# One more head of tile 0 as a streamed head, value rows one group later, paired forgetting scores and a fifth late head

## The reference

```
h   = x + W_out [ forgetting attention (8 heads of 64) || differential attention (4 heads of 2 x 64) ] (W_in RMSNorm(x))
h   = h + PEER(RMSNorm(h))
out = RMSNorm_final(h)

forgetting: softmax(q.k / 8 + c_q - c_k, causal) v,   c = cumsum(log sigmoid(f + b))
differential: (softmax(q1.k1 + alibi) - lambda softmax(q2.k2 + alibi)) v, chunk mask, RMSNorm of each head

PEER, for each block of 128 tokens, each of 8 heads:
  q  = xn @ w_q;  s1, i1 = top16(q1 . keys1);  s2, i2 = top16(q2 . keys2)
  16 best of the 256 sums  ->  expert numbers e (16 of 16384) and gates g = softmax(top)
  hid = gelu(u_tab[e] . xn) * g
  out += sum over the 16 of hid * v_tab[e]
```

## Time and profile before

| | |
|---|---|
| median of 3 runs | 1544.32 us |
| the profiled execution | 1543.67 us |
| its span | 1541.9 us |
| moved | 596.50 MB, 387 GB/s over the span |
| busy | PE 81%, DVE 71%, POOL 50%, ACT 30% |

### The profile page before, as it was taken

The page is one execution under the profiler, slowest core; times in us unless marked ns, Lnnn a source line. Parts: engine busy times, 40 slices in busy tenths (PEclk is TensorE's granted clock), DMA queues, the critical chain, the costliest instruction groups (busy, mean ns, idle before and its releaser), DMA issues.

```text
span 1541.9 us, 12952 instructions
## 1 busy us (share of the span) xinstructions
PE 1253.9 (81%) x3663; PEld 654.6 (42%) x3663; DVE 1097.3 (71%) x2538; ACT 459.2 (30%) x1188; POOL 771.6 (50%) x653
## 2 busy tenths in 40 slices
PE   9999978897787829899978777787787777878767
PEld 8776645574444514444433333333333233333323
DVE  3257799998998987666666676666666766666654
ACT  3432254446524312222222222222122322222222
POOL 0026587777568754345455444445544454444540
PEclk9999988898998959999999989989999999899998
DMA  9669899999899999999999999999999999999994
GB/s 385 258 254 414 341 322 367 372 382 318 277 363 337 401 388 422 421 422 421 421 423 421 422 421 422 422 421 422 421 422 421 422 421 421 421 422 421 421 421 182
DMA packets 102045, 596.50 MB, mean 387 GB/s; under 512 B 11736, under 2 KB 11736, under 8 KB 46680
## 3 DMA queue, kind: packets, MB, share of 16 engines
q0 software_dynamic: 92160, 536.91, 86.2%
q1 hardware_dynamic: 9816, 58.77, 9.5%
HBM read 593.54 MB, written 2.10 MB: 386 GB/s over the span
## 4 chain that ended last, share of the span: by engine, by line
DMA 39%; PE 16%; DVE 5%; POOL 2%; ACT 2%; issue 2%; DVEq 0%
PE acc L968 14%; DMA map_mem<-in_peer_uv_dram,eidx 8%; DMA v_all<-in_peer_uv_dram,eidx 8%; DMA mix_mem<-in_peer_uv_dram,eidx 6%; DMA u_ring<-in_peer_uv_dram,eidx 5%; DMA v_ring<-in_peer_uv_dram,eidx 4%; DMA w_ring<-in_peer_uv_dram,eidx 4%; DMA act_mem<-in_peer_uv_dram,eidx 3%; PE mm L764 1%; ACT diag L1202 1%; DVE map_mem L1521 1%; PE sc L764 1%; DVE v_all L1521 1%; POOL v_ring L685 1%; DMA v_ring<-in_peer_v_dram,eidx 1%
## 5 line engine op out<-in xcount | busy, mean ns | idle before, releaser
L1195 ACT ACTIVATE gel<-hid 128x4 f32<-128x4 f32 x126 | 25.9, 205 | 786.5 <-DVE hid L1521 686.3
L678 POOL DMA_INDIRECT u_ring<-in_peer_u_dram,eidx x128 | 157.4, 1230 | 173.7 <-DVE eidx L1501 98.5
L685 POOL DMA_INDIRECT v_ring<-in_peer_v_dram,eidx x128 | 155.1, 1212 | 60.9 <-issue 31.7
L968 PE MATMUL acc<-v_all,diag 128*128 128x512 f32 x240 | 123.5, 663 | 67.6 <-ACT diag L1202 35.7
L1549 DVE SCALAR_TENSOR_TENSOR h<-v_ring,coef,h 128x1024 f32<-128x1024 f32 x128 | 164.4, 1284 | 10.3 <-DMA v_ring<-in_peer_v_dram,eidx 6.9
L1513 DVE CUSTOM_DVE_ANT_0 u_ring<-u_ring,hn 128x1024 f32<-128x1024 f32 x128 | 155.9, 1218 | 20.1 <-DMA u_ring<-in_peer_u_dram,eidx 19.9
L968 PE MATMUL acc<-map_mem,diag 128*128 128x512 f32 x240 | 119.9, 647 | 24.6 <-ACT diag L1202 24.6
L968 PE MATMUL acc<-v_ring,diag 128*128 128x512 f32 x240 | 116.8, 632 | 25.9 <-ACT diag L1202 21.4
L968 PE MATMUL acc<-u_ring,diag 128*128 128x512 f32 x240 | 115.6, 627 | 27.0 <-ACT diag L1202 27.0
L1202 ACT ACTIVATE diag<-ident,coef 128x128 f32<-128x128 f32 x376 | 121.0, 390 | 33.3 <-DVE coef L1539 27.4
L699 POOL DMA_INDIRECT v_all<-in_peer_uv_dram,eidx x60 | 70.0, 1166 | 91.1 <-PE acc L968 85.3
(11 more groups left out here) (282 smaller groups left out, 2328.4 us busy)
## 6 DMA issues: line engine op xcount, KB each, us to landing
w_ring<-in_slabs_dram SPq DMA_DIRECT2D x29, 1024.0 KB, 8.2
v_ring<-in_slabs_dram SPq DMA_DIRECT2D x6, 1024.0 KB, 10.6
u_ring<-in_slabs_dram SPq DMA_DIRECT2D x6, 1024.0 KB, 10.9
map_mem<-in_slabs_dram SPq DMA_DIRECT2D x6, 1024.0 KB, 8.1
h<-in_x_dram SPq DMA_DIRECT2D x4, 512.0 KB, 12.5
u_ring<-in_peer_u_dram,eidx POOLq DMA_INDIRECT x128, 7.1
v_ring<-in_peer_v_dram,eidx POOLq DMA_INDIRECT x128, 7.3
v_all<-in_x_cols_dram SPq DMA_DIRECT2D x3, 512.0 KB, 7.4
```

The source lines that it names most:

```text
L678: nc.gpsimd.indirect_dma_start(out=u_ring[:, c % U_RING, :], out_offset=None, in_=peer_u[0], in_offset=bass.IndirectOffsetOnAxis(ap=eidx[n ...
L685: nc.gpsimd.indirect_dma_start(out=v_ring[:, c % V_RING, :], out_offset=None, in_=peer_v[0], in_offset=bass.IndirectOffsetOnAxis(ap=eidx[n ...
L968: last = nc.tensor.matmul(acc[half][:, :], diag[:, c % COLS, :], v_row(n, c)[:, half * BANK:(half + 1) * BANK], start=first, stop=(n % PH ...
L1195: nc.scalar.activation(gel[:, par, g0:g0 + COLS], hid[:, par, g0:g0 + COLS], ACT.Gelu).then_inc(gelu_done, 1)
```

## The change

- `HOSTS = 1` becomes `HOST_HEADS = 7`: the eighth head of tile 0 (n = 7) is a streamed head. Its v rows go to `acc` instead of `h`; `fin_tile` adds both as before, now at n = 8. Its first matmul starts the banks, so DVE no longer clears them; PE waits for what DVE waited for.
- `SLOTS` becomes 28. With the fifth late head out of the list, shares of 533.0 stand over 27 groups, 19.7 to a group.
- `BEHIND = 2`: DVE adds group k-2 beside the dots of group k, ACT does the GELU of group k-1 at gap 4 of group k, and POOL issues v rows four places later. DVE works the last two hosted groups of adds off in the first streamed group.
- The order of the places changes: six are free early (`FREE_ROWS`), and rows of n = 7 are gathered from the last hosted group on.
- Forgetting scores come in pairs at even steps: both 64-row matmuls, then both 40-row matmuls.
- `LATE_HEADS` = 5.

```diff
-HOSTS = 1
+HOST_HEADS = 7
-LATE_HEADS = 4
+LATE_HEADS = 5
+BEHIND = 2
-    SLOTS = HOSTS * PH * GRP
+    SLOTS = HOST_HEADS * GRP
...
-        row_mem = [m for flat in (v_flat, map_mem, ur_flat, vr_flat) for m in halves_of(flat)]
-        EARLY_ROWS = len(row_mem) - 4
+        row_mem = [m for flat in (v_flat, map_mem) for m in halves_of(flat)]
         row_mem += [store[:, 0:PH * 2 * K1], mix_mem[:, :]]
+        FREE_ROWS = len(row_mem)
+        row_mem += [m for flat in (ur_flat, vr_flat) for m in halves_of(flat)]
...
+        def group_at(k):
+            return k // GRP, k // GRP % 2, k % GRP * COLS
...  gather_row, POOL
-                elif place == EARLY_ROWS:
+                elif place == 0:
+                    pool.wait_ge(pv_done, len(item_list))
+                elif place == FREE_ROWS - 1:
+                    pool.wait_ge(mm_full, mm_done(("mixT", TILES - 1, 1)))
+                elif place == FREE_ROWS:
                     pool.wait_ge(dot_done, HOSTED)
+                elif place == FREE_ROWS + 2:
                     pool.wait_ge(v_used, HOSTED)
...  POOL's order
+            for n in range(HOST_HEADS):
                 for c in range(TOPK):
                     ahead = TOPK * n + c + COLS
                     if ahead < HOSTED:
                         ...
                         gather_u(ahead // TOPK, ahead % TOPK)
-                    gather_v(n, c)
+                    elif ahead - HOSTED < FREE_ROWS:
+                        if ahead == HOSTED:
+                            numbers_of(HOST_HEADS)
+                        gather_row(HOST_HEADS, ahead - HOSTED)
+                    if TOPK * n + c >= (BEHIND - 1) * COLS:
+                        gather_v(*divmod(TOPK * n + c - (BEHIND - 1) * COLS, TOPK))
+            for c in range(COLS, FREE_ROWS):
+                gather_row(HOST_HEADS, c)
+            for i in range(HOSTED - (BEHIND - 1) * COLS, HOSTED):
+                gather_v(*divmod(i, TOPK))
...  PE
+            def pair_scores(g, step):
+                t, first = at_step(g, 0, step)
+                nk, j = P * (t + 1), GROUPS[g].index(t)
+                if first == 0:
+                    pe.wait_ge(selq_ready, 2 * (t + 1))
+                both = [(HD * (m % 2), m // 2, map_no[(t, m)]) for m in (first, first + 1)]
+                for lo, ch, k in both:
+                    if k >= len(sc_b):
+                        pe.wait_ge(sc_drained, k + 1 - len(sc_b))
+                    nc.tensor.matmul(sc_b[k % len(sc_b)][:, 0:nk], qT[lo:lo + HD, ...], kv_t[lo:lo + HD, ...],
+                                     start=True, stop=False)
+                for lo, ch, k in both:
+                    nc.tensor.matmul(sc_b[k % len(sc_b)][:, 0:nk], selq[lo:lo + 40, ...], caug[lo:lo + 40, 0:nk],
+                                     start=False, stop=True).then_inc(sc_full, 1)
...  first streamed group, PE
-                    first = n % PH == 0 and c == 0
-                    if first:
+                    first = (n == HOST_HEADS or n % PH == 0) and c == 0
+                    if first and n == HOST_HEADS:
+                        pe.wait_ge(*emptied(MM[MM_HOSTED - 1]))
+                        ...
+                        pe.wait_ge(sc_drained, len(map_list))
+                    elif first:
                         pe.wait_ge(acc_drained, 2 * (n // PH))
...  ACT, hosted
-                            if gap == 2 * COLS - 2:
-                                gelu(n, n % 2, grp * COLS)
+                        if gap == COLS and (n or grp):
+                            gelu(*group_at(GRP * n + grp - 1))
...  DVE, hosted
-                        behind = ((k - 1) // GRP, (k - 1) // GRP % 2, (k - 1) % GRP * COLS)
+                    behind = group_at(k - BEHIND)
...
-                for half in range(2):
-                    link(nc.vector.memset(acc[half][:, :], 0.0))
...  DVE, first streamed group
+                    if n == HOST_HEADS and grp == 0:
+                        for k in range(GRP * HOST_HEADS - BEHIND, GRP * HOST_HEADS):
+                            behind = group_at(k)
+                            coefs(*behind)
+                            for c in range(COLS):
+                                if k == GRP * HOST_HEADS - BEHIND:
+                                    row_dot(n, par, c)
+                                add_row(behind[0], behind[1], behind[2] + c)
```

More of the change, by code:

```diff
@@ L459, in build @@
         place_rows, places = {}, []
-        for i in range((HEADS - PH * HOSTS) * TOPK):
+        for i in range((HEADS - HOST_HEADS) * TOPK):
             if i < FULL_FROM:
@@ L571, in slab_view @@
             return w.rearrange("p (c n) -> p c n", c=KC)
[L573 removed]
+        HOSTED = HOST_HEADS * TOPK
         def row_place(n, c):
@@ L711, in _ @@
                 gather_u(0, c)
-            for n in range(PH * HOSTS):
+            for n in range(HOST_HEADS):
                 for c in range(TOPK):
@@ L977, in _ @@
                 piece(*p_)
[L978 to L984, removed]
+            for n in range(HOST_HEADS):
+                for grp in range(GRP):
+                    for gap in range(GAPS):
+                        for p_ in pieces_in(n, grp, gap):
+                            piece(*p_)
+            for n in range(HOST_HEADS, HEADS):
                 for grp in range(GRP):
                     peer_group(n, grp * COLS)
-                    k = GRP * (n - PH * HOSTS) + grp
+                    k = GRP * (n - HOST_HEADS) + grp
                     if k in LATE_PE:
@@ L1238, in _ @@
             gate_exp(0)
[L1239 to L1242, removed]
-                            if gap == 2 * COLS - 2:
-                                gelu(n, n % 2, grp * COLS)
-                            for p_ in pieces_in(n, grp, gap):
-                                piece(*p_)
-                        if tile and n == PH * tile and grp == 0:
-                            fin_rt(tile - 1)
-                        if grp == 2:
-                            gate_exp(n + 1)
-            for n in range(PH * HOSTS, HEADS):
+            for n in range(HOST_HEADS):
+                for grp in range(GRP):
+                    for gap in range(GAPS):
+                        if gap == COLS and (n or grp):
+                            gelu(*group_at(GRP * n + grp - 1))
+                        for p_ in pieces_in(n, grp, gap):
+                            piece(*p_)
+                    if grp == 2:
+                        gate_exp(n + 1)
+            gelu(*group_at(GRP * HOST_HEADS - 1))
+            act.wait_ge(tr_full, len(item_list))
+            for n in range(HOST_HEADS, HEADS):
                 for grp in range(GRP):
@@ L1687, in _ @@
-            for n in range(PH * HOSTS, HEADS):
+            for n in range(HOST_HEADS):
+                par = n % 2
+                for grp in range(GRP):
+                    k = GRP * n + grp
+                    behind = group_at(k - BEHIND)
+                    for gap in range(GAPS):
+                        c = gap // 2
+                        if grp == 1:
+                            topk_second(n + 1, 1 - par, gap)
+                        elif gap == GAPS - 1:
+                            next_head(n, par, grp)
+                        if gap % 2 == 0 and gap < GAPS - 1:
+                            dot(n, par, grp * COLS + c)
+                        elif gap < GAPS - 1 and k >= BEHIND:
+                            if c == 0:
+                                coefs(*behind)
+                            add_row(behind[0], behind[1], behind[2] + c)
+                        for p_ in pieces_in(n, grp, gap):
+                            piece(*p_)
```

83 lines of the change are left out of this document (28 added, 55 removed).

## The result

The changed kernel takes 1550.94 us in the median of 12 runs (1548.02 to 1556.04), the kernel before 1544.38 us (12 runs): the ratio is 1.0042, 95% interval [1.0031, 1.0053]. It is 6.5 us slower. Forecast were 1538 us and 70% for faster. The profiled execution took 1548.74 us, its span is 1546.9 us, 5.0 more than before (the sum had -6.1); so it is again 1.8 us around the span.

The account below looks back on a forecast made before the run. The bound was taken to change by stage: PE early, DVE from 200 to 488.7 us, DMA bytes in the stream. Terms -7.1 - 2.5 + 1 + 2.5 gave -6.1 us, median about 1538 us, range 1533 to 1542 (8 in 10: 1529 to 1548).

Parts of the forecast that it names:

- C, the mark itself: Time of the first 8 KB row, set against 488.73 us before: +1 us, with -5 and +10 as ends.
- over 15 us of waits for PE: DVE from 200 us to the first 8 KB row: a few us forecast; more than 15 would refute the +1 us.
- The credit for four adds fewer: DVE's adds before the first 8 KB row: -4.8 us if DVE alone sets the time, mostly spent waiting for PE.
- B: Bytes left behind the first 8 KB row: +5.0 us of rows, -7.5 us of slabs, together -2.5 us, or 0.
- D, the seam: Passage from hosted to streamed rows: 0.9 us for slow v rows, 1.6 us more for waits; +2.5 us, ends 0 and +6.
- A: Last hosted head, 488.7 to 558.4 us: streamed at 421 GB/s, its 69.7 us would take 62.6, so -7.1 us.
- The early stage: Start of hosting: PE's projections end at 193.8 us, first scores not before 195.5, so most of DVE's 4.8 us is waited away.
- More: DVE sets the whole hosted stage, first 8 KB row 4.8 us earlier, seam under 1 us: -13.5 us, 1531 us; chance 0.22.
- The slower rival: Paired scores bind PE to DVE's drains, first 8 KB row 10 us late, dry seam: +6.4 us, 1550 us; chance 0.12.
- No change: Tail gain given back: streamed rows no faster than 378 GB/s, or first 8 KB row 7 us late; 1544 us; chance 0.14.
- PE's 12 us of late head: Fifth late head in the stream: hidden under DMA time over five more groups; without that cover, at most 12 us.
- ACT's GELU: Hosted stage: moving it costs nothing and removes ACT's 100.2 us of waiting; counted only as cover for the denser list.

Follow-up runs that it names:

- b_dense: b_rows with the hosted pieces spread over the first 27 of its 32 groups, 20.4 shares a group: 1559.08 us, ratio 1.0092.
- b_rows: The kernel before with only the new order of places, six free places and POOL's interleaved first rows: 1542.69 us, ratio 0.9983.
- c1: The changed kernel with value rows one group behind and four late heads: 1548.59 us, ratio 1.0021.
- c2: The changed kernel with value rows one group behind, four late heads and unpaired forgetting scores: 1548.16 us, ratio 1.0015.
- a_behind1: The changed kernel with value rows one group behind and the GELU at the end of its group: 1544.74 us, ratio 1.0002.
- h8: The changed kernel with eight hosted heads, four late heads and DVE clearing the two banks in the first streamed group: 1549.64 us, ratio 1.0025.
- a_ff: The changed kernel with the forget gates of tiles 1 to 3 at the head of PE's projections: 1550.73 us, ratio 1.0034.
- a_unpair: The changed kernel with forgetting scores one head at a time, as before the change: 1551.78 us, ratio 1.0048.
- b_pair: The kernel before with the paired forgetting scores alone: 1545.1 us, ratio 1.0000.
- a_late4: The changed kernel with four late heads instead of five: 1546.97 us, ratio 1.0016.

## Why the prediction was wrong

- **C, the mark itself, is the step that failed.** +1 us was forecast, with an upper end of 10; measured is 8.4 us (497.1 against 488.7), which is 7.4 of the 11.1 us by which the sum missed the span. Of it 1.8 us stand before place 24, 9.3 us in the stretch, and 2.7 us are won back behind it. The premise was that from the first scores on DVE's work is the same and that PE at 87% stays out of its way. Both loads came as forecast (DVE 271 us; PE 254 us in the stretch, forecast 252), but DVE's idle time rose by 9 us.
- **What took the time in the stretch.** b_dense changes the list's density alone, and the stretch goes from 286.7 us at 17.8 shares a group (b_rows) to 301.4 at 20.4, with waits for PE and ACT; c1 and c2, with head 7 moved, have 303.5 and 302.0 at 20.4, and a_behind1 has 294.8 at 19.7. An average of 87% is no cover where single pieces are waited for. In the changed kernel the waits are others: row data 7.9 us (before 0.3), PE 8.3 us (5.3), ACT 3.4 us (4.9). C had nothing for row data, and its own sign, over 15 us of waits for PE, did not come. The lag is not what brings them at this density, for a_behind1 has 7.7 us too. No run changes the density alone at lag two, so for the changed kernel density is the likely cause and not a shown one: h8, at 17.8, passes place 108 at 486.0 us, the changed kernel, with head 7 moved and 19.7, at 494.8.
- **The credit for four adds fewer** (-4.8 us as the lower end of C, mostly spent in the forecast) was worth at most 2.6 us at the first row (499.7 to 497.1), and against it stood the price that the sum did count in B, +5.0 us. Taken together the lag was a loss by my own numbers, and I did not say so, because I mixed it with the slabs.
- **D, the seam, was mis-sized, inside its ends.** I took 2.5 us (0 to 6) with "about 5 us of rows in hand" behind the last add. (Eight v rows at 378 instead of 421 GB/s are 1.1 us, not 0.9.) After the first 8 KB row 69.7 us run at 395 GB/s, a loss of 4.3 us against 0.3 with lag one. A and D together were forecast at -4.6 us and came to -2.8 us (4.3 against the 7.1 lost before).
- **B** held in its parts: three slabs are issued behind the mark, as forecast, and a fourth just before it, at 494.6 us, which lands behind it, so B lies between -2.5 and 0. The sum, 8.4 - 2.8 and this, is 3.1 to 5.6 us; the span grew by 5.0. Each term lies inside the ends that I gave it; the range of 1533 to 1542 us was narrower than those ends allow.
- **A was right as a mechanism**: in a_behind1 head 7 is streamed at 416 to 422 GB/s where it was hosted at 378. The changed stream has the same 421 GB/s. The Trainium skill ("DMA: Bandwidth & Descriptors", section "Measured (HBM→SBUF, 128 partitions, SWDGE, issued from GpSimd)") has 425 GB/s for a single core's 16 MB transfer, and the trace agrees with that figure, not with the 358 that the prediction weighed.
- **The early stage** was right: place 24 is passed at about the same time in all kernels with seven hosted heads (200.8 to 203.0 us against 199.4), so the four adds fewer gave no lead there. That PE's line of projections is what holds it, as the prediction said, isn't shown (a_ff); the first scores came at 192.6 us, where 195.5 was its estimate.
- **The rivals.** "More" needed DVE to be the only bound; h8 speaks against it, where a lead of 6.5 us at place 24 was gone at place 108. The slower rival (1550 us, given 0.12) has the time that came, and nearly the sum: a mark 10 us late and a dry seam. But its cause was the pairs, and a_unpair and b_pair show them to be neutral, so that its number fits is luck. The warning of the Trainium skill ("TensorEngine Tiling (Array Packing)", section "Gotcha 1: PSUM Pressure") found no price here, with three banks for scores: 0.06% between the ratios of a_unpair and the changed kernel. "No change" (0.14) had a late mark of 7 us, which did come (8.4), and the seam made it more than no change. PE's 12 us of late head stayed hidden in the stream, as forecast: 421 GB/s from 600 us on.
- **ACT's GELU** was called free cover. Up to 480 us its move took ACT's waits for it from 84.7 to 4.4 us (100.2 us up to 550 in the earlier trace rows). Together with the lag this helped the first row only where the list was denser than in the change (c1 to a_late4).

What stays open: what fixes the stretch at 292 to 294 us for every kernel with lag two or three, at 17.8, 19.7 and 20.4 shares alike; why at 19.7 shares DVE waits 7.7 to 7.9 us for row data, and at 20.4 only 0.5 to 2.2 us; and about half of the fifth late head's price.

## What to carry to other kernels

Put a price on a deeper software lag where the pipeline ends: here every step of lag added its transfers behind the seam and held buffers there, and it pays only if something upstream waits for what it delays. When work is packed denser beside a busy engine, average utilisation does not tell the cost; compress the list alone in a test, and read the length of a stretch in which the busy engine's own work is fixed. Shortening the largest wait of a trace may gain nothing, since the next wait can take up what was won: try it before believing it.

## What the runs showed of the hardware

The clock paid for part of the denser work. From 200 to 300 us PE was busy for 99.3 us in b_dense at a granted clock of 0.98; in b_rows, with gaps, it was 88.9 us at 0.89:

```profile
200.00:300.00 100.00, 88.88 (x324) 52.47 (x320) 95.30 (x201) 49.16 (x107) 75.40 (x62) 0.89 0.95 352
```

Busy time times clock, an estimate of the work at full speed, is 97 against 79 us, so b_dense did more of it there than the busy shares tell. And in the tail of the hosted stage 4 KB rows, with four weight slabs among them, left bandwidth unused with the DMA engines busy: 378 GB/s at a share of 0.98, where b_rows has 416 at 1.02 from 540 to 560 us, mostly with 8 KB rows. The rate of such a mixture isn't fixed: from 125 to 186 us it was 403 GB/s at 1.00.
